# Memory keys and values in three float32r passes, with the memory transposes inside the last input group

## The reference

```python
h = x
y = mixers(rms_norm(h, norm_mix) @ w_in)     # w_in: 2048 x (13*512 + 16)
h = h + groupnorm(y) @ w_out
mem_n = rms_norm(mem, norm_mem)              # 256 memory rows
k, v = mem_n @ wk, mem_n @ wv                # 2048 x 2048 each
h = h + attention(rms_norm(h, norm_cross) @ wq, k, v) @ wo
h = h + moe(rms_norm(h, norm_ffn))           # 32 experts, top 2
out = rms_norm(h, norm_final)
```

## Time and profile before

| | |
|---|---|
| median of 3 runs | 2186.67 us (2182.43 to 2187.85) |
| profiled execution, its own time | 2189.37 us |
| span of the profiled execution | 2187.6 us |
| TensorE matmul busy | 2005.4 us (92%) |
| VectorE, ScalarE, GpSimd busy | 565.8, 476.4, 44.5 us |
| HBM read | 553.51 MB, 254 GB/s over the span |

### The profile page before, as it was taken

One profiled execution on the slowest core, in us unless ns is written; L12 is line 12 of the kernel. 1 busy time (PEld: TensorE's weight loads), 2 busy tenths in 40 slices (PEclk: granted clock), 3 DMA queues, 4 the chain that ended last, 5 costly groups with the idle time before them and its releaser, 6 DMA issues.

```text
span 2187.6 us, 24683 instructions
## 1 busy us (share of the span) xinstructions
PE 2005.4 (92%) x10000; PEld 1309.8 (60%) x10000; DVE 565.8 (26%) x896; ACT 476.4 (22%) x684; POOL 44.5 (2%) x54
## 2 busy tenths in 40 slices
...
GB/s 235 165 105 173 135 155 173 98 100 130 110 112 164 78 192 149 159 78 191 282 51 357 415 404 405 407 413 416 403 417 403 414 383 400 418 410 413 407 215 42
DMA packets 134603, 556.61 MB, mean 254 GB/s; under 512 B 15392, under 2 KB 15624, under 8 KB 84232
## 3 DMA queue, kind: packets, MB, share of 16 engines
...
q0 software_dynamic: 1024, 2.10, 1.3%
...
HBM read 553.51 MB, written 2.10 MB: 254 GB/s over the span
## 4 chain that ended last, share of the span: by engine, by line
PE 59%; issue 22%; DMA 15%; DVE 2%; SPq 1%; ACT 1%; POOL 0%; ACTq 0%; DVEq 0%; POOLq 0%
DMA arena<-in_moe_w_dram 15%; PE ps L834 13%; PE ps L857 10%; PE ps L845 6%; PE ps L545 5%; PE ps L540 4%; PE ps L523 3%; PE ps L525 3%; PE ps L524 3%; PE ps L517 1%; PE ps L518 1%; PE ps L519 1%; PE ps L809 1%; PE ps L931 1%; PE ps L675 1%
## 5 line engine op out<-in xcount | busy, mean ns | idle before, releaser
L834 PE MATMUL ps<-arena 128*64 128x512 f32 x2048 | 513.2, 646 | 71.5 <-DMA arena<-in_moe_w_dram 69.5
L834 PEld LDWEIGHTS ps<-arena 128*64 128x64 f32 x2048 | 147.4, 147 | 382.4 <-issue 252.3
L1327 DVE TENSOR_TENSOR w_lo<-arena,w_hi 128x1024 fp32r<-128x1024 f32 x200 | 235.6, 1222 | 273.7 <-ACT w_hi L986 273.4
L986 ACT ACTIVATE w_hi<-arena 128x1024 fp32r<-128x1024 f32 x200 | 200.2, 1051 | 334.8 <-PE ps L519 168.6
L857 PE MATMUL ps<-arena 128*64 128x512 f32 x1024 | 227.7, 597 | 0.5 <-DVE arena L1798 0.5
L857 PEld LDWEIGHTS ps<-arena 128*64 128x64 f32 x1024 | 73.7, 138 | 148.6 <-issue 147.9
L517 PE MATMUL ps<-x_hi,w_hi 128*128 128x256 f32 x512 | 147.6, 288 | 10.1 <-DVE w_lo L1327 10.1
L518 PE MATMUL ps<-x_lo,w_hi 128*128 128x256 f32 x512 | 146.8, 287 | 0.0
L519 PE MATMUL ps<-x_hi,w_lo 128*128 128x256 f32 x512 | 146.7, 287 | 0.0
L845 PEld LDWEIGHTS ps<-stack,arena 128*128 128x128 f32 x512 | 121.9, 328 | 26.3 <-issue 26.3
L845 PE MATMUL ps<-stack,arena 128*128 128x64 f32 x512 | 126.6, 402 | 0.0
...
## 6 DMA issues: line engine op xcount, KB each, us to landing
...
```

Of the source, the lines that this page charges most:

```text
L834: last = mm(ps[rows_, m, :], xe[:, ECH * i + c, :], ring_up[m][i][:, c, :], start=(i == 0 and c < 2), stop=(i == ECH - 1 and c >= 2))
L986: fn(hi_ring[(2 * n + u) % 4][:], ring_a[i][:, 2 * u:2 * u + 2, :], ACT.Copy).then_inc(S["w_hi"], 1)
L1327: V.tensor_tensor(w_lo[i][:, 2 * u:2 * u + 2, :], ring_a[i][:, 2 * u:2 * u + 2, :], hi_ring[(2 * n + u) % 4][:].bitcast(F32), ALU.subtract ...
```

## The change

- **Keys and values** of the memory run in `dense_split`, with `mem` transposed into `m_hi` and `m_lo`. ScalarE and VectorE get `high` and `low` of these 32 chunks, placed in the HGRN2 steps (`high_of`, `low_of`) and in the attention steps.
- **Last input group**: DFT along features after its chunk 0, memory transposes around chunk 2.
- **Start**: `x` comes first, in two halves, into a buffer of its own (`x0`); transposes and splitting alternate with the chunks of group 0; `mem` is loaded after group 0's weights and squared behind group 0. `h` is loaded later.
- **Gates**: `wg` is split too; 48 float32r matmuls give the 16 gates feature-major over 256 tokens; four matmuls, now behind group 4, sort them.
- **rsqrt**: one Sqrt on ScalarE, then a reciprocal and the Newton step in three instructions on VectorE. `squares` calls for the Sqrt table beforehand.
- **HGRN2's start**: Abs, Exp, Ln, Exp are taken for both directions at once; `decay(0)` stands ahead of two group norms.
- **`w_out`**: `y` is transposed from feature 0 on before the last group norm is done, in turn with the chunks of its first group.

```diff
-     G_WO: (at_r("y_hi", 136, [P, KT, T]), at_r("y_lo", 64, [P, KT, T])),
+     "mem": (at_r("m_hi", 96, [P, KT, T]), at_r("m_lo", 128, [P, KT, T])),
+     G_WO: (at_r("y_hi", 136, [P, KT, T]), at_r("y_lo", 96, [P, KT, T])),
...
-return (g * NCH + i, w_hi[0]) if g < G_IN else ((g - G_WO + G_IN) * NCH + i, w_hi[1])
+return g * NCH + i, w_hi[0 if g < G_WO else 1]
...
+for j in range(NT):
+    sp.dma_start(x0[:, j, :], ins["x"][0, j * P:(j + 1) * P, :]).then_inc(S["x_half0" if j == 0 else "x_half1"], 16)
 sp.dma_start(ident[:], ins["c_eye"]).then_inc(S["eye_in"], 16)
...
-sp.dma_start(h, ins["x"][0].rearrange("(j p) d -> p j d", p=P)).then_inc(S["x_in"], 16)
 sp.dma_start(ffn_gain[:], ins["norm_ffn"][0].rearrange("(p k) -> p k", k=KT)).then_inc(S["ffn_in"], 16)
-sp.dma_start(mem, ins["mem"][0].rearrange("(j p) d -> p j d", p=P)).then_inc(S["mem_in"], 16)
...
+        sp.dma_start(mem, ins["mem"][0].rearrange("(j p) d -> p j d", p=P)).then_inc(S["mem_in"], 16)
         sp.dma_start(mixc, ins["c_mix"]).then_inc(S["cmix_in"], 16)
         sp.dma_start(arena(188.25, 5 * 256), ins["c_dft"]).then_inc(S["cdft_in"], 16)
         sp.dma_start(hmask_f, ins["c_masks"]).then_inc(S["cmask_in"], 16)
...
-sp.wait_ge(S["chunk_used"], G_IN * NCH)
+load_dense(G_WO)
+sp.wait_ge(S["chunk_used"], G_WO * NCH)
 sp.dma_start(h, ins["x"][0].rearrange("(j p) d -> p j d", p=P)).then_inc(S["x_in"], 16)
-for g in range(G_WO, G_XO + 4):
+for g in range(G_WO + 1, G_XO + 4):
     load_dense(g)
...
+def turned_split(n, chunk):
+    pe.wait_ge(S["ts_hi"], n * (KT // 2) + CH // 2 * (chunk + 1))
+    pe.wait_ge(S["ts_lo"], n * (KT // 2) + CH // 2 * (chunk + 1))
...
-pe.wait_ge(S["x_in"], 16)
+for j in range(NT):
+    pe.wait_ge(S["x_half0" if j == 0 else "x_half1"], 16)
+pe.wait_ge(S["cols_act"], 1)
 pe.wait_ge(S["diag_dve"], 1)
-turn_split(0, h, [diag[:, j, :] for j in range(NT)])
-turned_split(0)
+x_scales = [diag[:, j, :] for j in range(NT)]
+turn_split(0, x0, x_scales, part=range(4))
+for i in range(NCH):
+    turned_split(0, i)
+    dense_split(0, W_IN[0][1], split[G_IN], part=[i])
+    if i < 2:
+        turn_split(0, x0, x_scales, part=(2 * i + 4, 2 * i + 5))
...
 for g, (name, fm, _, _) in enumerate(W_IN):
-    dense_split(g, fm, split[G_IN])
+    if 1 <= g < G_IN - 1:
+        dense_split(g, fm, split[G_IN])
...
-        pe.wait_ge(S["wg_in"], 16)
-        for j in range(NT):
-            for k in range(KT):
+        pe.wait_ge(S["wg_lo"], 1)
+        for k in range(KT):
+            mm(ps[0:16, 4, 0:T], wg_hi[:, k, :], x_hi[:, k, :], start=(k == 0), stop=False)
+            mm(ps[0:16, 4, 0:T], wg_hi[:, k, :], x_lo[:, k, :], start=False, stop=False)
+            last = mm(ps[0:16, 4, 0:T], wg_lo[:, k, :], x_hi[:, k, :], start=False, stop=(k == KT - 1))
         last.then_inc(S["gate_pe"], 1)
+    if g == 4:
         pe.wait_ge(S["gate_dve"], 1)
         for kind in range(4):
-            for j in range(NT):
-                last = mm(ps[0:NH, 5 + kind // 2, (kind % 2) * T + j * P:(kind % 2) * T + (j + 1) * P],
-                          gtok[:, j, kind * NH:(kind + 1) * NH], ident[:], start=True, stop=True)
+            last = mm(ps[0:NH, 5 + kind // 2, (kind % 2) * T:(kind % 2 + 1) * T],
+                      ident[0:16, kind * NH:(kind + 1) * NH], g16, start=True, stop=True)
         last.then_inc(S["gate_pe"], 1)
...
     if G_ML - 1 <= g < G_ML - 1 + NH:
         ml_scores(g - G_ML + 1)
 pe.wait_ge(S["cdft_in"], 16)
-pe.wait_ge(S["proj_a"], G_IN)
-pe.wait_ge(S["proj_b"], G_IN)
+pe.wait_ge(S["proj_a"], G_IN - 1)
+pe.wait_ge(S["proj_b"], G_IN - 1)
 pe.wait_ge(S["ml_y"], NH)
 pe.wait_ge(S["ml_den"], 2 * NH)
 for j in range(NT):
...
 pe.wait_ge(S["mem_in"], 16)
 pe.wait_ge(S["diag_dve"], 2)
+m_scales = [diag[:, j, :] for j in range(NT)]
+turn_split(1, mem, m_scales, part=range(4))
+last_in(2)
+turn_split(1, mem, m_scales, part=range(4, 8))
+last_in(3)
+turned_split(1, NCH - 1)
 for j in range(NT):
...
     w, lev = s // HG_LEVELS, s % HG_LEVELS
     g, c = G_WK + (s + HG_LEAD) // NCH, (s + HG_LEAD) % NCH
...
-        dense(G_WV + c // NCH, False, memT, part=[c % NCH])
+        dense_split(G_WV + c // NCH, False, split["mem"], part=[c % NCH])
...
-pe.wait_ge(S["y_done"], 4)
-turn_split(1, y, [ident[:]] * 2)
-turned_split(1)
-for n in range(4):
+pe.wait_ge(S["y_done"], 3)
+pe.wait_ge(S["na_y"], 16)
+turn_split(2, y, [ident[:]] * 2, part=range(4))
+for i in range(NCH):
+    turned_split(2, i)
+    dense_split(G_WO, False, split[G_WO], part=[i])
+    if i == 1:
+        pe.wait_ge(S["y_done"], 4)
...
-def squares(src, to=None):
+def squares(src, to=None, halves=()):
+    sqrt_table()
...
 def rsqrt(w):
     calls[0] += 1
     act.wait_ge(S["var_dve"], calls[0])
-    step(fn(st[:, 16:16 + w], st[:, 8:8 + w], ACT.Ln))
-    fn(st[:, 24:24 + w], st[:, 16:16 + w], ACT.Exp, scale=-0.5).then_inc(S["rs_act"], 1)
+    fn(st[:, 16:16 + w], st[:, 8:8 + w], ACT.Sqrt).then_inc(S["rs_act"], 1)
...
+act.wait_ge(S["eye_in"], 16)
+squares(x0, flat(ps[:, 4:8, :]), ("x_half0", "x_half1"))
+rsqrt(NT)
 act.wait_ge(S["cols_pe"], 1)
 fn(cols[:], ps[:, 0, 0:104], ACT.Copy).then_inc(S["cols_act"], 1)
 act.wait_ge(S["cols_act"], 1)
-act.wait_ge(S["x_in"], 16)
-squares(h)
-rsqrt(NT)
-act.wait_ge(S["mem_in"], 16)
-act.wait_ge(S["diag_dve"], 1)
-squares(mem)
-turned_hi(0, split[G_IN][0], 0)
-rsqrt(NT)
+high(0, (0,))
+turned_hi(0, split[G_IN][0], 0, part=range(4))
+high(0, (1,))
+turned_hi(0, split[G_IN][0], 0, part=range(4, 8))
+high(0, (2, 3))
...
+    if g == 1:
+        act.wait_ge(S["mem_in"], 16)
+        act.wait_ge(S["ts_lo"], KT // 2)
+        squares(mem, flat(ps[:, 4:8, :]))
+        rsqrt(NT)
...
+    if g == G_IN - 1:
+        act.wait_ge(S["fn_pe"], 1)
+        fn(fa[:, 0].rearrange("p g c n -> p (g c n)"), flat(ps[:, 4:6, :]), ACT.Copy).then_inc(S["fn_act"], 1)
+        high(g, (2,))
+        turned_hi(1, split["mem"][0], 3, part=range(4))
+        high(g, (3,))
+        turned_hi(1, split["mem"][0], 3, part=range(4, 8))
+        high(G_WK, (0,))
+act.wait_ge(S["ml_y"], NH)
+gates_f = [flat(buf[name]) for name in ("hff", "hfb")]
+for w in range(2):
+    fn(flat(htmp[w]), gates_f[w], ACT.Abs).then_inc(S["hp_act"], 1)
+for w in range(2):
+    act.wait_ge(S["hp_act"], w + 1)
+    fn(flat(htmp[w]), flat(htmp[w]), ACT.Exp, scale=-1.0).then_inc(S["hp_act"], 1)
+high(G_WK, (1,))
+for w in range(2):
...
+high(G_WK, (2,))
+for w in range(2):
     act.wait_ge(S["hp_dve"], w + 1)
-    fn(f, flat(htmp), ACT.Exp).then_inc(S["hp_act"], 1)
+    fn(gates_f[w], flat(htmp[w]), ACT.Exp).then_inc(S["hp_act"], 1)
+high(G_WK, (3,))
 for _ in range(2):
     rsqrt(NT)
+def high_of(c):
+    if c < 2 * KT:
+        high(G_WK + c // NCH, (c % NCH,))
 for s in range(2 * HG_LEVELS):
     act.wait_ge(S["h_sub"], s + 1)
     fn(flat(he[s % 2]), flat(he[s % 2]), ACT.Exp).then_inc(S["h_exp"], 1)
+    high_of(s + HG_LEAD + 1)
...
+    for c in NA_CHUNKS[m][1:]:
+        high_of(KT + c)
...
+act.wait_ge(S["na_o"], NA_H // 2 * NT)
+act.wait_ge(S["na_y"], 16)
+high(G_WO, (0,))
+turned_hi(2, split[G_WO][0], 4, part=range(4))
+high(G_WO, (1,))
+turned_hi(2, split[G_WO][0], 4, part=(4, 5))
 rsqrt(NT)
+high(G_WO, (2,))
+turned_hi(2, split[G_WO][0], 4, part=(6, 7))
+high(G_WO, (3,))
...
     dve.wait_ge(S["rs_act"], calls[0])
+    step(V.reciprocal(r, root))
     step(V.tensor_tensor(t_, r, r, ALU.mult))
-    step(V.tensor_tensor(t_, t_, var, ALU.mult))
-    step(V.tensor_scalar(t_, t_, -0.5, 1.5, ALU.mult, ALU.add))
-    step(V.tensor_tensor(r, r, t_, ALU.mult))
+    step(V.scalar_tensor_tensor(t_, t_, -0.5, var, ALU.mult, ALU.mult))
+    step(V.scalar_tensor_tensor(r, t_, 1.5, r, ALU.add, ALU.mult))
...
+    if g == 1:
+        dve.wait_ge(S["ts_pe"], KT // 2)
+        row_scale()
...
+    if g == G_IN - 1:
+        dve.wait_ge(S["ml_y"], NH)
+        dve.wait_ge(S["silu_act"], 3)
+        step(V.tensor_tensor(yml, yml, buf["mo"], ALU.mult))
+        dve.wait_ge(S["fn_pe"], 1)
+        V.tensor_copy(fa[:, 1].rearrange("p g c n -> p (g c n)"), flat(ps[:, 6:8, :])).then_inc(S["fn_dve"], 1)
+        low(g, (2,))
+        turned_lo(1, split["mem"][1], split["mem"][0], 3, part=range(4))
+        low(g, (3,))
+        turned_lo(1, split["mem"][1], split["mem"][0], 3, part=range(4, 8))
+        low(G_WK, (0,))
+low(G_WK, (1,))
+dve.wait_ge(S["ts_pe"], KT)
+step(V.tensor_copy(y[:, :, 0:GW], yml))
...
+    if w == 0:
+        low(G_WK, (2,))
...
-group_norm(0)
-group_norm(2)
...
 decay(0)
+low(G_WK, (3,))
+group_norm(0)
+dve.wait_ge(S["fn_act"], 2)
+dve.wait_ge(S["fn_dve"], 2)
+dve.wait_ge(S["y_done"], 1)
+group_norm(2)
...
+    low_of(s + HG_LEAD + 1)
...
+    for c in NA_CHUNKS[m][1:]:
+        low_of(KT + c)
     dve.wait_ge(S["na_p"], 2 * m + 2)
     V.reciprocal(st[:, 44:46], st[:, 54:56]).then_inc(S["na_r"], 1)
+    low_of(KT + NA_CHUNKS[m][-1] + 1)
...
+low(G_WO, (0,))
+turned_lo(2, split[G_WO][1], split[G_WO][0], 4, part=range(4))
+low(G_WO, (1,))
+turned_lo(2, split[G_WO][1], split[G_WO][0], 4, part=(4, 5))
```

(23 more changed lines are left out.)

148 lines of the change are left out of this document (63 added, 85 removed).

## The result

The changed kernel takes 2093.06 us (median of 4 runs, 2087.86 to 2095.86) against 2187.26 us measured beside it: ratio 0.9569, 95% interval 0.9545 to 0.9594. The forecast was 2092 us, between 2080 and 2118. The profiled execution took 2092.59 us, its span is 2090.7 us; that of before took 2189.37 us, with a span of 2187.6.

The account below looks back on a forecast made before the run. It took DMA to bound the experts and TensorE the HGRN2 steps and attention, with TensorE waits elsewhere. Terms summing to 94.7 us took the median from 2186.7 to 2092 us, range 2080 to 2118.

Parts of the forecast that it names:

- Keys, values, attention: Cheaper split chunks save 17.6 us in the HGRN2 steps and 16.6 us in the attention.
- Helpers bind: Rival, chance 0.2: VectorE's load and slow spells hold HGRN2 steps at 8.69 us and take a third of attention's gain; 2115 us.
- Gates: Gate matmuls: 5.8 us for 48 at full clock, 1.7 for four float32 ones; 21.5 us saved.
- Start: Kernel start to group 0's end: earlier x, shorter rsqrt and transposes among chunks save 11.3 us, bounds 7 to 13.
- The thin cover at group 1: Third chunk of group 1: its rest is ready 1.3 us before TensorE arrives; without this cover 1 to 4 us lost.
- starved: Rival, chance 0.1: small loads in SyncE's queue delay group 1's first chunk, losing the 11.3 us at the beginning; 2103 us.
- Into HGRN2: Stretch before the first HGRN2 product: cheaper key chunks and shorter rsqrts save 6 us; the gap keeps about 7.
- the walk: Step-by-step times up to the first HGRN2 product: norms end at 67.3, Exp at 68, GpSimd last at 71.1 us.
- The serial rival: Rival, chance 0.03: VectorE and GpSimd wait for each other, HGRN2 steps run in series at 15.3 us; 2209 us.
- Tables: Rival, chance 0.05: Sqrt's table adds a 1.28 us load at each of nine norms; 2104 us.
- w_out and last group: Interleaved transposes save 12.5 us at w_out, bounds 9 and 14; removed gaps save 3.4 us in the last input group.
- Experts: Expert stretch unchanged in length; at the kernel's end both table loads and one function go, 2.8 us.

Follow-up runs that it names:

- The single undo: Changed kernel with keys and values of the memory in one float32 matmul instead of three float32r passes, weight splitting kept: 2130.08 us, ratio 0.9751.
- The series run: Changed kernel with w_out's last group norm first, then all its input transposes, then the first product: 2103.1 us, ratio 0.9618.
- the Ln and Exp one: Changed kernel with the inverse root as Ln then Exp again, no Sqrt and no early load of its table: 2114.19 us, ratio 0.9674.

## Why the prediction was right

**Keys, values, attention.** Both terms hold within 0.6 us. The single undo (34.1 us in the trace for 34.2 forecast) shows that the passes are the cause and that the helpers add nothing. The steps came as forecast too: 7.54 us for 7.57, 15.24 for 15.3.

**Helpers bind (0.2).** Not in this kernel, but nearer than "1.9 us of slack a step": VectorE is busy 71.49 of 91.00 us, so 1.6 us a step, and one more operation cost 11 us. The estimate of the busy time (5.7 us, measured 5.9) was good; what I missed is where slack is spent, at the exit.

**Gates.** Right in sum and in both parts: 5.62 us for 5.8, at full clock as chosen, and the sorting 1.9 for 1.7.

**Start.** 9.3 for 11.3, inside 7 to 13. The steps came as written, each a little late: first split matmul at 20.38 (19.6), third chunk at 38.93 (37.7), group 0's end at 51.88 (50.3). The diagonal was 0.3 us late, the transposes took 5.75 for 5.3, the way to the third chunk 0.45 more, and the fall to half clock behind its wait cost 1.4 us (12.95 for two chunks of 5.79) where I added 1. The rest is the reckoning: before, group 0 ended at 61.15 and not 61.4, and 61.4 less 50.3 is 11.1, not 11.3. The thin cover at group 1 held; starved it was not.

**Into HGRN2.** 4.5 for 6. A part of that stands in the stage before, which gained 1.0 us more than forecast: together 8.9 for 9.4. What failed is the end of the walk. Exp and GpSimd came near their times (410.6 and 412.2, where the walk gives 410.0 and 413.1), but the gap kept 7.75 us because VectorE was last, and not GpSimd: behind the norms came the copy of the first product (L1610, 1.28 us), which the walk doesn't name, and `decay` of the next step, then `queries`, which ends at 413.9; so the first product came 0.9 us late. The first instruction of `decay` took 1.69 us beside a product on GpSimd, 0.68 us otherwise:

```profile
410.70 1.50 POOL L436 TENSOR_TENSOR arena<-arena 128x512 f32<-128x512 f32 x1 [409.61 <-ACT arena L1120]
```

```profile
411.06 1.69 DVE L1566 TENSOR_TENSOR arena<-arena 128x512 f32<-128x512 f32 x1
```

VectorE's subtraction began 0.36 us behind the product and ended 0.55 us behind its end. That agrees in kind with the lock that the Trainium skill, SBUF — State Buffer, section "SBUF: two separate sides", describes. The serial rival (0.03) found no support: GpSimd's 16 products take 1.89 us on average, and a step stays at 7.54 us.

**Tables (0.05).** Refuted: undoing Sqrt costs 21 us or more. The sizes of the parts on the path (1.48 a norm) were right, their effect at the entry into the attention was not.

**w_out and last group.** 12.3 and 4.4 for 12.5 and 3.4. The series run shows the first; no run undoes the new start or the new last group, so their times are read from the stages alone. Behind `w_out` the group norm was late by 0.92 us, for about 1 forecast.

**Experts.** 2.8 forecast and 7.2 read. At the end no table load is left in the last norm: from VectorE's scaled mean square to the scaling of the output it takes 1.2 us (2082.91 to 2084.11) where it was 3.8 (2177.12 to 2180.92). The other 4 us can't be told from chance: among the twelve profiled kernels with the same code from there on (all but before and the Ln and Exp one) the rest of the span is 1038.2 to 1049.7 us, and before's is 1049.9. That the sum came out within 1 us is therefore partly luck: the terms before the experts made 89.7 us where I had 91.9.
